# Prologue of a hybrid convolution/GLA layer: order of transposes, first modulation sums and two loads

## The reference, cut to what matters here

```python
def layer(x, c, ...):
    mod = jax.nn.silu(c) @ w_ada + b_ada
    sh1, sc1, g1, sh2, sc2, g2 = jnp.split(mod, 6, axis=-1)
    h = rmsnorm(x, norm_pre1) * (1 + sc1[:, None]) + sh1[:, None]
    proj = h @ w_in
    ...            # short conv branch, GLA branch, merge
    x = x + g1[:, None] * rmsnorm(merged @ w_out, norm_post1)
    ...            # channel sub-layer: w_up, conv, gelu, w_down
```

## Time and profile before

| what | us |
|---|---|
| median of 3 runs | 1013.62 |
| lowest, highest | 1010.78, 1016.25 |
| profiled execution | 1020.51 |
| its span in the trace | 1018.8 |

### The profile page before, as it was taken

One profiled execution on the slowest core, in us unless ns is written; L12 is line 12 of the kernel. 1 busy time (PEld: TensorE's weight loads), 2 busy tenths in 40 slices (PEclk: granted clock), 3 DMA queues, 4 the chain that ended last, 5 costly groups with the idle time before them and its releaser, 6 DMA issues.

```text
span 1018.8 us, 18829 instructions
## 1 busy us (share of the span) xinstructions
PE 994.4 (98%) x7799; PEld 902.0 (89%) x7799; DVE 544.0 (53%) x876; ACT 385.9 (38%) x592; POOL 230.9 (23%) x124
## 2 busy tenths in 40 slices
PE   5999999999899999999999999999999999999997
PEld 4789889988799999999998889999999999888886
DVE  2321104566266575355345588877777778750204
ACT  3552533143243234425444255333333334533212
POOL 2043433243144333233254020000000000013330
PEclk9999999999899999999999999999999999999999
DMA  9555333486354646445437023222332232322222
GB/s 331 187 104 164 118 90 96 136 112 137 96 163 117 158 126 168 48 124 158 109 130 232 1 70 98 83 84 84 101 87 84 83 84 63 124 62 88 82 66 93
DMA packets 145029, 115.61 MB, mean 113 GB/s; under 512 B 11225, under 2 KB 121585, under 8 KB 144945
## 3 DMA queue, kind: packets, MB, share of 16 engines
q1 hardware_dynamic: 144273, 113.85, 41.3%
q10 hardware_dynamic: 672, 0.56, 0.2%
HBM read 107.02 MB, written 7.35 MB: 112 GB/s over the span
## 4 chain that ended last, share of the span: by engine, by line
PE 95%; issue 1%; DVE 1%; DMA 1%; ACT 1%; SPq 1%; DVEq 0%; ACTq 0%
PE pair L1948 50%; PE pair L2046 16%; PE pair L2368 10%; PE pair L2321 5%; PE pair L2127 2%; PE pair L2100 1%; PE pair L1938 1%; PE pair L1878 1%; PE pair L1883 1%; DMA ada_first<-in_w_ada 1%; PE pair L2038 1%; PE pair L2190 1%; PE pair L2179 1%; PE pair L2039 1%; PE pair L2040 1%
## 5 line engine op out<-in xcount | busy, mean ns | idle before, releaser
L1948 PE MATMUL pair<-h_hi,w_hi 128*128 128x288 f32 x1280 | 286.7, 302 | 0.1
L1948 PE MATMUL pair<-h_hi,w_lo 128*128 128x288 f32 x1280 | 279.9, 296 | 0.0
L1948 PE MATMUL pair<-h_lo,w_hi 128*128 128x288 f32 x1280 | 279.8, 296 | 0.0
L881 POOL TENSOR_TENSOR w_lo<-raw,w_hi 128x1024 fp32r<-128x1024 f32 x55 | 135.1, 2459 | 556.3 <-ACT w_hi L960 556.3
L1948 PEld LDWEIGHTS pair<-h_hi,w_hi 128*128 128x128 f32 x1280 | 208.3, 189 | 20.0 <-issue 18.3
L1948 PEld LDWEIGHTS pair<-h_lo,w_hi 128*128 128x128 f32 x1280 | 208.6, 189 | 0.0
L1948 PEld LDWEIGHTS pair<-h_hi,w_lo 128*128 128x128 f32 x1280 | 208.4, 189 | 0.0
L960 ACT ACTIVATE w_hi<-raw 128x1024 fp32r<-128x1024 f32 x66 | 69.3, 1056 | 151.9 <-PE pair L2040 75.6
L881 POOL TENSOR_TENSOR w_lo<-raw_c,w_hi 128x1024 fp32r<-128x1024 f32 x24 | 70.3, 2938 | 132.3 <-ACT w_hi L960 132.3
L2046 PE MATMUL pair<-w_hi,f_hi 128*128 128x512 f32 x176 | 68.9, 392 | 0.0
L2046 PE MATMUL pair<-w_lo,f_hi 128*128 128x512 f32 x176 | 68.7, 390 | 0.0
(11 more groups left out here) (352 smaller groups left out, 1638.1 us busy)
## 6 DMA issues: line engine op xcount, KB each, us to landing
raw_c<-in_w_ada SPq DMA_DIRECT2D x32, 512.0 KB, 4.9
raw<-in_w_in SPq DMA_DIRECT2D x224, 64.0 KB, 3.6
raw_c<-in_w_in SPq DMA_DIRECT2D x192, 64.0 KB, 3.8
raw<-in_w_up SPq DMA_DIRECT2D x24, 512.0 KB, 4.9
raw<-in_w_down SPq DMA_DIRECT2D x22, 512.0 KB, 3.8
raw_up<-in_w_up SPq DMA_DIRECT2D x20, 512.0 KB, 3.8
ada_first<-in_w_ada SPq DMA_DIRECT2D x16, 512.0 KB, 12.3
raw<-in_w_in SPq DMA_DIRECT2D x8, 512.0 KB, 4.7
```

The source lines that it names most:

```text
L881: pool.tensor_tensor(lo, raw_tile(n)[:, :], hi.bitcast(F32), ALU.subtract).then_inc(S("w_lo_done"), 1)
L1948: ins = pe.matmul(bank[pair][:, half, 0:HALF], w[:, i, :], x[:, i, HALF * half:HALF * half + HALF], start=i == 0 and p == 0, stop=i == KT ...
```

## The change

1. SP no longer issues the four `raw_in0` chunks (4 to 7 of `raw01`) between the row blocks of half 1; the eight row blocks of half 1 follow each other. ACT issues these chunks instead, between its copies of the third and the fourth token tile.
2. The first 36 fillers become 18, and they now stand behind the wait for `c_split`.
3. The transposes of token tiles 0, 1 and 2 come ahead of the first modulation block; blocks 0 to 3 of half 0 follow, then tile 3, blocks 4 and 5, tile 4, blocks 6 and 7. No filler stands between them.
4. Blocks 6 and 7 of half 1 and `first_back(1)` come ahead of the low-activation pass over channels 0 to 3, and the 16 fillers behind `first_back(1)` go. In all 64 fillers go.

```diff
@@ block.sync
-            for i in range(4):
-                load_ada_first(1, i)
-            for i in range(4, KT):
-                sp.dma_start(raw01[:, i, :], w_in[P * i:P * i + P, IN_K:IN_K + 2 * DK]).then_inc(S("raw_in0"), 16)
-            for i in range(4, KT):
+            for i in range(KT):
                 load_ada_first(1, i)
@@ block.scalar
-            for i in range(4):
-                act.dma_start(raw01[:, i, :], w_in[P * i:P * i + P, IN_K:IN_K + 2 * DK]).then_inc(S("raw_in1"), 16)
+            def load_first_tiles(half):
+
+                for i in range(4 * half, 4 * half + 4):
+                    act.dma_start(raw01[:, i, :], w_in[P * i:P * i + P, IN_K:IN_K + 2 * DK]) \
+                       .then_inc(S("raw_in0" if half else "raw_in1"), 16)
+
+            load_first_tiles(0)
             for t in range(TT):
+                if t == 3:
+                    load_first_tiles(1)
                 n = ROWS[t]
                 act.wait_ge(S("x_tr"), t + 1)
@@ block.tensor
-            keep_warm(36)
             pe.wait_ge(S("c_split"), 3)
-            for i in range(3):
+            keep_warm(18)
+            for t in range(3):
+                x_to_channels(t)
+            for i in range(4):
                 ada_first_rows(0, i)
-                keep_warm(6)
-            for t in range(TT):
-                x_to_channels(t)
-                ada_first_rows(0, 3 + t)
-                if t < TT - 1:
-                    keep_warm(3)
+            x_to_channels(3)
+            for i in (4, 5):
+                ada_first_rows(0, i)
+            x_to_channels(4)
+            for i in (6, 7):
+                ada_first_rows(0, i)
             parameters()
             first_back(0)
             keep_warm(16, 7)
@@ low passes over channels 0 to 3
+            ada_first_rows(1, 6)
+            ada_first_rows(1, 7)
+            first_back(1)
             for i in range(4):
                 pe.wait_ge(S("h_lo_done"), i + 1)
                 for n in range(2):
                     first_product(2, i, n)
-            ada_first_rows(1, 6)
-            ada_first_rows(1, 7)
-            first_back(1)
-            keep_warm(16, 7)
```

## The result

The changed kernel takes 1003.7 us (median of 6 runs, 1002.0 to 1004.9) where the kernel before takes 1014.64 us (6 runs, 1010.8 to 1016.3): 10.9 us less, ratio 0.9886, 95% interval 0.9860 to 0.9913. Forecast were 7.0 us less, 1006.6, with a range from 1003.5.

What follows compares the result with a forecast made beforehand. PE, holding 95% of the chain, was taken as the bound. Half 0's order saves 6.2 us, the gate gives back 1.2, the reorder saves 2.1: 7.1, say 7.0, so 1013.6 becomes 1006.6, range 1003.5 to 1012.0.

Steps and rivals of the forecast that it cites:

- The step that failed: Everything behind the prologue: PE's list unchanged, its semaphores earlier by as much, so the rest was costed at nothing.
- Up to `first_back(0)`: Half 0 of the prologue: `first_back(0)` at 25.7 where it was 31.94, 6.2 us earlier (5.3 to 7).
- then the landing at 23.3 ends last: Half 0, all at full clock: blocks 6 and 7 landing at 23.3 set the end, 24.5 instead of 26.4.
- ACT's four issues: Ahead of ACT's copies of tiles 3 and 4: four moved DMA issues take 1.8 us and cost nothing.
- The gate of block 3: Half 1, ahead of blocks 0 and 1: block 3 lands at 30.9, giving back 1.2 of the 6.2 us.
- One more stretch at half clock: Second rival, in the prologue: 3.3 us at 0.50 costs 1.7 us, gain 5.3, time 1008.3; chance 0.14.
- Hole closed, blocks 6 and 7 of half 1 in time: Transfers from 28.5 to 32.5: the 2.3 us lost at 165 GB/s vanish, blocks land at 36.8, no wait.
- the first rival: Transfers keep old times or worse, the 2.3 us hole stays: gain 5.7 or 4.7, 1007.9 or 1008.9; chance 0.22.
- Reorder at half 1: Behind `first_back(1)`: the low-activation pass replaces 2.1 us of fillers and idling, saving 2.1 us.
- The rule on transposes and the clock: Skill's rule, weighed at the first tiles: transposes don't engage full clock; the prediction held the trace's fillers contradict it.
- The third rival: Clock stays low through the prologue without the fillers: product near 60, 11 us slower, 1024.5; chance 0.05.
- Prologue in all: Start to the product on channels 4 to 7: at 42.1 instead of 49.17, 7.1 us earlier.

Runs made afterwards that it cites:

- 64 more: 64 small idle transposes added at the head of PE's list: changed kernel 1007.65 us against 1003.7, kernel before 1011.07 us against 1015.1.
- both pairs of equal length: Changed kernel plus 64 small transposes against kernel before: 1007.65 against 1015.1 us; changed plus 128 against before plus 64: 1003.65 against 1011.07 us.
- 128 more: Changed kernel with 128 small idle transposes added at the head of PE's list: 1003.65 us against 1003.7.
- the chunks behind the fifth copy: Changed kernel with ACT's four chunks issued behind its fifth tile copy instead of behind the third: 1002.19 us.
- the undone first part: Changed kernel with SP again issuing the four chunks between blocks 3 and 4 of half 1, ACT none: 1005.36 us.
- 2 fillers: Changed kernel with its fourth part undone and 16 of the 18 first fillers taken out, list length kept: 1005.73 us.

## Why the prediction was right in sign and short in size

- **The step that failed** is the sentence "From there on PE's list is the same [...] I cost the rest at nothing". PE's list is the same behind the prologue, but its position in the code loads is not. The trace of the kernel before had the sign: 5.3 us of "issue" waits in a kernel whose PE has hardly another wait after 60 us. I read only the first 50 us, and had no rival for a change of length. The term put at nothing measures 4.0 us in medians (64 more in either kernel: +3.95 and -4.0), in the profiled execution of before 5.3 plus half clock. Without it the change is worth 7.4 us, in both pairs of equal length, where 7.0 were forecast.
- **Up to `first_back(0)`**: forecast 25.7, measured 25.28. The working was off by two terms that cancel: the clock was already full for the first tiles (16 transposes in 1.97 us), so PE stood ready at 22.4 and waited 1.20 us for blocks 6 and 7, which landed 0.3 later than the prediction's 23.3. This was the branch "then the landing at 23.3 ends last". That the two cancel is luck. The fillers were read wrongly too: PE's wait for `c_split` ended at 9.01 and not at 8.3, DVE's copy into `c_wide` having taken 0.83 us for 0.20, so they ran until 13.1 and the pause ahead of the tiles was 1.44 us instead of some 2.4. And the 26.4 beside the 25.3 in that passage comes out of no step of its own.
- **ACT's four issues**: 1.78 us, forecast 1.8, and free, as said.
- **The gate of block 3**: forecast 30.9, measured 31.3. The term that was missing stands behind it: from 30.9 to 34.2 the clock was granted at half, so that blocks 0 and 1 took 1.94 us for 1.07 and the next product 1.27 for 0.80. One more stretch at half clock was a rival of its own (0.14), and it occurred in the profiled execution; from the gate to the product it took 43.43 - 31.33 = 12.1 us, in three others without it 10.8 (42.77 - 32.01 with 64 more; 43.30 - 32.52 with 128 more; 41.56 - 30.78 with the chunks behind the fifth copy). So 1.3 us that the forecast 7.1 lost in this trace are the clock's. In how many executions that happens isn't known.

```profile
30.90:34.20 3.30, 2.87 (x20) 1.60 (x21) 2.33 (x4) 0.00 (x0) 0.00 (x0) 0.50 1.05 387
```

- **Hole closed, blocks 6 and 7 of half 1 in time**: right. They are worked on from 39.4 on behind no wait, at 396 GB/s from 28.5 to 32.5 where it had been 165. The hole did not stay, as the first rival had it, and the undone first part shows what it was worth.
- **Reorder at half 1**: forecast 2.1, measured 2.0 and 2.2 in medians, 2.6 and 2.4 in traces.
- **The rule on transposes and the clock**: in the changed kernel nothing but transposes had run since 9.01, and the first tiles were at full speed. The third rival (the clock stays low through the prologue) had no support in any run: where the tiles were slow, in three traces, they were at full speed again from tile 3 on, at 21.5 at the latest.
- **Prologue in all**: 7.1 forecast, 5.74 in the trace, about 7 without the half clock. With lists of equal length the whole change gave 7.4 in medians. So for the prologue alone the sum was sound, and the 1003.7 us came about by a second cause that the sum didn't have.

## What to carry to other kernels

Before costing an edit at nothing behind its own stretch, read the list of PE's waits over the whole span: an "issue" wait inside a run of equal short instructions was a boundary between code loads here, and an edit that changes the number of instructions ahead of it, even a filler in idle time, moved the kernel's time by 4 us either way. To compare two versions of an early stage, keep the instruction count of the engine the same modulo one load (here by idle small transposes), or the comparison measures the boundary as well. And where several loads feed one gate, the order within the queue decides: four late-needed DMAs ahead of or beside the needed ones cost 1.5 to 2.5 us here.

## What was not expected of the hardware

- Code loads can cost time on PE when they meet short work: 0.2 to 3.2 us each, ten of the eleven in or just behind runs of 64 matmuls that take 0.74 us, with a period that fits 256 PE instructions (128 transposes more restore the time, 16, 32 and 64 don't). The Trainium skill, "Runtime: NRT & Kernel Launch", section "Instruction fetch mechanics", gives the blocks of 256 instructions, with which all lists here agree; it calls the crossing "mostly hidden", which holds for nearly all of the 61 or 62 loads of these kernels and fails at two of them in the kernel before, by 2.0 and 3.2 us. A stall ended 2.2 to 2.6 us after its load began, in all eleven; what makes a load begin late stays open.
- TensorE's clock differs from execution to execution: behind the 18 fillers the first tiles ran at full speed in seven traces, in which PE had been idle for 1.44 to 1.83 us ahead of them, and slowed to half in two, with 1.95 and 2.38 us (also with 2 fillers and 4.86 us). That is a difference of up to 1.2 us at `first_back(0)`, and the half clock behind the gate is one of 1.3 us. Whether the pause is the cause was not tested. A trace's prologue is not to be read finer than that.
- Four DMAs of 128 KB between the 512 KB ones of the same queue went with 4 us at 159 to 200 GB/s; the same four on another queue (396), or behind in the same one (386), did not.
